# Second layer's feed-forward: seventeen weight panels as seven half-size products instead of eight, sums on GpSimd

## The reference

```python
D_FF_2 = 2816            # 22 panels of 128 gate and 128 value columns

def swiglu(t, w_in, w_out):
    a, b = jnp.split(t @ w_in, 2, axis=-1)
    return (jax.nn.silu(a) * b) @ w_out

x = x + g2 * swiglu(modulate(rmsnorm_2(x, norm2_g[i]), sh2, sc2), ffn_w_in[i], ffn_w_out[i])
```

## Time and profile before

| | |
|---|---|
| median of three runs | 2506.89 us (2505.44 to 2507.58) |
| the profiled execution | 2507.14 us, span 2505.8 us |
| TensorE busy | 2472.0 us, 99% of the span |
| VectorE, ScalarE busy | 1508.1 us (60%), 988.9 us (39%) |
| GpSimd busy | 136.7 us (5%) |
| mean granted clock of TensorE | 0.996 |

### The profile page before, as it was taken

How to read it: one execution, slowest core, us unless ns; L and a number is a source line. 1 busy time by engine, 2 the same in 40 slices (tenths; PEclk the granted TensorE clock), 3 DMA queues, 4 the chain that set the end, 5 groups by cost and what they waited for, 6 DMA issues and landing times.

```text
span 2505.8 us, 32300 instructions
## 1 busy us (share of the span) xinstructions
PE 2472.0 (99%) x13178; PEld 2052.0 (82%) x13178; DVE 1508.1 (60%) x2618; ACT 988.9 (39%) x1985; POOL 136.7 (5%) x148
## 2 busy tenths in 40 slices
PE   8999999999999999999999999999999999999998
PEld 6888888778888788888888788888888888888887
DVE  8787753555666557766665288676644644633434
ACT  6543242453354442333522377432223423422222
POOL 1000000000010010000122000100000001000001
PEclk9999999999999999999999999999999999999999
DMA  4221012212333144654212100366632222222222
GB/s 148 85 84 35 18 52 93 93 68 76 126 135 124 62 185 169 235 202 151 93 67 85 51 1 18 141 226 230 221 113 87 102 101 94 92 101 101 97 84 72
DMA packets 39941, 270.33 MB, mean 108 GB/s; under 512 B 4336, under 2 KB 4592, under 8 KB 9072
## 3 DMA queue, kind: packets, MB, share of 16 engines
q1 hardware_dynamic: 30064, 206.71, 23.0%
q0 software_dynamic: 9040, 60.33, 6.6%
q10 hardware_dynamic: 688, 1.22, 0.1%
HBM read 266.14 MB, written 2.10 MB: 107 GB/s over the span
## 4 chain that ended last, share of the span: by engine, by line
PE 94%; DVE 4%; ACT 2%; issue 0%; DMA 0%; DVEq 0%; ACTq 0%; POOLq 0%
PE bank L142 91%; PE bank L145 2%; DVE w_lo L151 1%; ACT tmp L148 0%; DVE dd L151 0%; DVE x_t L159 0%; DMA kept_consts<-in_consts 0%; DVE tmp L151 0%; DVE change L159 0%; ACT w_hi L148 0%; ACT da_p L148 0%; ACT L148 0%; DVE dd L145 0%; DVE da_stat L168 0%; DVE low L151 0%
## 5 line engine op out<-in xcount | busy, mean ns | idle before, releaser
L142 PE MATMUL bank<-h_hi,w_hi 128*128 128x512 f32 x1824 | 694.5, 395 | 0.1
L142 PE MATMUL bank<-h_lo,w_hi 128*128 128x512 f32 x1824 | 677.1, 390 | 0.0
L151 DVE TENSOR_TENSOR w_lo<-w_raw,w_hi 128x512 fp32r<-128x512 f32 (+3 forms) x746 | 490.8, 713 | 140.0 <-ACT w_hi L148 139.5
L142 PE MATMUL bank<-h_hi,w_lo 128*128 128x512 f32 x1824 | 570.7, 390 | 0.0
L148 ACT ACTIVATE w_hi<-w_raw 128x512 fp32r<-128x512 f32 (+3 forms) x746 | 426.6, 637 | 334.9 <-PE bank L142 321.3
L142 PEld LDWEIGHTS bank<-h_lo,w_hi 128*128 128x128 f32 x1824 | 342.2, 188 | 72.4 <-DVE h_lo L159 0.8
L142 PEld LDWEIGHTS bank<-h_hi,w_hi 128*128 128x128 f32 x1824 | 342.4, 188 | 70.2 <-issue 0.8
L142 PEld LDWEIGHTS bank<-h_hi,w_lo 128*128 128x128 f32 x1824 | 341.4, 188 | 68.2
L142 PE MATMUL bank<-f_hi,w_hi 128*128 128x512 f32 x816 | 315.6, 390 | 0.2 <-DVE w_lo L151 0.2
L142 PE MATMUL bank<-f_lo,w_hi 128*128 128x512 f32 x816 | 300.1, 389 | 0.0
L142 PE MATMUL bank<-f_hi,w_lo 128*128 128x512 f32 x816 | 270.3, 389 | 0.0
(11 more groups left out here) (383 smaller groups left out, 3004.4 us busy)
## 6 DMA issues: line engine op xcount, KB each, us to landing
w_raw<-in_pack_ffn SPq DMA_DIRECT2D x60, 1024.0 KB, 4.8
ada_w<-in_ada_w POOLq DMA_DIRECT2D x48, 1024.0 KB, 5.1
w_raw<-in_pack_mlp SPq DMA_DIRECT2D x32, 1024.0 KB, 4.9
w_raw<-in_pack_gdn_qkv SPq DMA_DIRECT2D x12, 1024.0 KB, 4.7
w_raw<-in_pack_sc_cu SPq DMA_DIRECT2D x8, 1024.0 KB, 4.7
w_raw<-in_pack_ffn SPq DMA_DIRECT2D x8, 768.0 KB, 4.2
w_raw<-in_pack_gdn_z SPq DMA_DIRECT2D x4, 1024.0 KB, 4.7
w_raw<-in_pack_gate_a SPq DMA_DIRECT2D x4, 1024.0 KB, 4.8
```

Source lines behind the costliest of these rows:

```text
L142: return self.engine.matmul(*a, **k) if self.engine is not None else self
L151: return self.engine.tensor_tensor(*a) if self.engine is not None else self
```

## The change

In panels 5 to 21 of the second layer's first product, the block product of a 2 x 2 arrangement (row blocks 0 to 3 and 4 to 7, gate and value columns, first and second 256 tokens) is formed from seven products of half size (`m1` to `m7`), in the manner of Strassen and Winograd, where the plain form has eight. Each is four row blocks by three matmuls of 256 columns, into one half of a PSUM bank; four banks serve a panel. The weights' seven forms are the four quarters that occur as they are (the first piece of 1024 columns holds two, the second of 512 one) and four sums, made by GpSimd in `w_sums` (`seven_sums_pool`) and split like the others: six pieces in place of four. The input's sums `t_sums` are made once, by GpSimd (`seven_forms_pool`), and split into `t_hi` and `t_lo` by ScalarE and VectorE during panels 1 to 3. The four quarters of the result are put together by adds: five on VectorE from PSUM, two on GpSimd, two copies on ScalarE. The hidden tile of a panel is finished during the next one. The plain panels 0 to 4 and the whole first layer stay as they were.

```diff
+    PIECES, SEVEN_PIECES, SEVEN_FROM = 4, 6, 5
...
+        if j == 0:
+            parts = [w[n % 2][:, 0:2 * T].rearrange("p (k m) -> p k m", k=DT) for w in (w_hi, w_lo)]
+            return raw[:, :, 0:P], parts
...
+    def seven_lo_piece(V, n, j):
+        src, (hi, lo) = seven_piece(n, j)
+        V.wait_ge(*at("act_hi", (n, j)))
+        V.tensor_tensor(lo, src, hi.bitcast(F32), ALU.subtract).then_inc(
...
+    def seven_sums_pool(G, n, before):
...
+        for j, (out, a, b, op) in enumerate(((s1, a21, a22, ALU.add), (s2, s1, a11, ALU.subtract),
+                                             (s3, a11, a21, ALU.subtract), (s4, a12, s2, ALU.subtract))):
+            if before is not None:
+                G.wait_ge(*at("dve_lo", (before, j + 2)))
...
+        if i == SEVEN_FROM:
+            T_.wait_ge(*at("dve_seven", ("t", 3)))
+        T_.wait_ge(*at("dve_lo", n))
...
+            for k in range(4):
+                T_.matmul(out, hi[:, k, :], b_hi(k), start=(k == 0), stop=False)
+                T_.matmul(out, lo[:, k, :], b_hi(k), start=False, stop=False)
+                done = T_.matmul(out, hi[:, k, :], b_lo(k), start=False, stop=(k == 3))
...
+    def seven_forms_pool(G):
+        a, b = sq[0], sq[1]
+        for k in range(4):
+            for t, tile in ((a, k), (b, 4 + k)):
+                G.wait_ge(*at("act_h_hi", ("ffn1", tile)))
+                G.wait_ge(*at("dve_h_lo", ("ffn1", tile)))
...
+                G.tensor_tensor(t[:, :], h_hi[:, tile, :].bitcast(F32), h_lo[:, tile, :].bitcast(F32), ALU.add).then_inc(
...
+            if k:
+                G.wait_ge(*at("dve_seven", ("t", k - 1)))
+            G.tensor_tensor(t_sums[:, 0, :], a[:, second_half], a[:, first_half], ALU.subtract).then_inc(
...
+            if behind is not None:
+                corner(behind)
+            piece()
+            if behind is not None:
+                product(behind)
+            add(i, "u2", s1, "m6", "b", 0, u2, at("act_seven", ("s1", i)), *made)
+            piece()
+            if behind is not None:
+                rest(behind)
+            piece()
+            add(i, "c11", s1, "m2", "c", 0, seven_a[:, first_half])
+            piece()
+            add(i, "u3", u2, "m7", "d", 0, u3, at("dve_seven", ("u2", i)), *made, frees=True)
+            piece()
+            piece()
+            add(i, "c21", u3, "m4", "b", 1, seven_b[:, first_half], at("dve_seven", ("u3", i)), frees=True)
...
+        for i, following in zip(SEVEN, SEVEN[1:] + [None]):
+            beside_it = following is not None and block_of(following) == block_of(i)
+            if beside_it:
+                seven_sums_pool(G, seven_n(following), seven_n(i))
+            corners(i)
```

More of the change, by code:

```diff
@@ L468, in panel_size, with in_seven, pieces_of, form_of @@
         return nk * width
-    PIECES = 4
+    PIECES, SEVEN_PIECES, SEVEN_FROM = 4, 6, 5
+    def in_seven(n):
+        return n < len(order) and order[n][0] == "ffn1_1" and order[n][2] >= SEVEN_FROM
+    def pieces_of(n):
+        return SEVEN_PIECES if in_seven(n) else PIECES
+    def form_of(parts, n, j):
+        whole, more = parts
+        if j < 4:
+            return whole[n % 2][:, T * j:T * (j + 1)]
+        return more[n % 2][:, j - 4, :]
+    def seven_piece(n, j):
+        raw = w_raw[n % 2][:, :].rearrange("p (k m) -> p k m", k=DT)
+        if j == 0:
+            parts = [w[n % 2][:, 0:2 * T].rearrange("p (k m) -> p k m", k=DT) for w in (w_hi, w_lo)]
+            return raw[:, :, 0:P], parts
+        parts = [form_of(w, n, j + 1) for w in ((w_hi, more_hi), (w_lo, more_lo))]
+        if j == 1:
+            return raw[:, 4:8, P:2 * P], [part.rearrange("p (k m) -> p k m", k=4) for part in parts]
+        return w_sums[j - 2][:, :], parts
@@ L591, in gemm_beside @@
                 for k in range(nk):
-                    if piece is not None and steps < PIECES:
+                    if piece is not None and steps < pieces_of(ahead):
                         piece(lane, ahead, steps)
@@ L3362, in hidden_before, with seven_place @@
         return ("pe_tile", (f"ffn1_{layer}", 0, 0, 1))
+    SEVEN_BLOCKS = [[i for i in range(max(k0, SEVEN_FROM), k0 + nk)] for k0, nk in FFN_BLOCKS]
+    SEVEN = [i for panels in SEVEN_BLOCKS for i in panels]
+    seven_n = lambda i: number["ffn1_1", 0, i]
+    block_of = lambda i: i // 8
+    hidden_of = lambda i: (1, i // 8, i % 8)
+    first_half, second_half = slice(0, HT), slice(HT, T)
+    def seven_place(place, i, half):
+        return bank_of((place, i))[:, HT * half:HT * (half + 1)]
@@ new lines, in seven_scalar, with tanh, hidden, piece @@
+    def seven_scalar(S, panels):
+        def tanh(i):
+            S.wait_ge(*at("dve_seven", ("c12", i)))
+            S.wait_ge(*at("dve_ffn", ("lo", *hidden_of(i - 1))))
+            S.activation(seven_y[:, :], seven_a[:, :], ACT.Tanh, scale=0.5).then_inc(*up("act_seven", ("tanh", i)))
+        def hidden(i):
+            layer, blk, f = hidden_of(i)
+            S.wait_ge(*at("dve_ffn", ("product", layer, blk, f)))
+            S.wait_ge(*at(*hidden_before(layer, blk)))
+            S.activation(f_hi[:, f, :], seven_y[:, :], ACT.Copy).then_inc(*up("act_ffn", ("hi", layer, blk, f)))
+        for i in panels:
+            ahead, before = seven_n(i) + 1, seven_before(i)
+            pieces = iter(range(pieces_of(ahead)))
+            def piece():
+                j = next(pieces, None)
+                if j is not None:
+                    split_hi_piece(S, ahead, j)
+            behind = None if i == panels[0] else i - 1
+            piece()
+            if behind is not None:
+                tanh(behind)
+            S.wait_ge(*(at("dve_seven", ("c12", before)) if before else at("dve_ffn", ("lo", 1, 0, i - 2))))
+            S.wait_ge(*at("pe_tile", ("m1", i)))
+            S.activation(s1, seven_place("a", i, 0), ACT.Copy).then_inc(*up("act_seven", ("s1", i)))
+            piece()
+            if behind is not None:
+                hidden(behind)
+            piece()
+            piece()
+            if before is not None:
+                S.wait_ge(*at("pool_seven", ("c22", before)))
+            S.wait_ge(*at("pe_tile", ("m5", i)))
+            S.activation(s5, seven_place("a", i, 1), ACT.Copy).then_inc(*up("act_seven", ("s5", i), frees=("a", i)))
+            piece()
+            piece()
+        tanh(panels[-1])
+        hidden(panels[-1])
@@ new lines, in seven_vector, with add, corner, product @@
+    def seven_vector(V, panels):
+        def add(i, name, left, product, place, half, out, *waits, frees=False):
+            V.wait_ge(*at("pe_tile", (product, i)))
+            for wait in waits:
+                V.wait_ge(*wait)
+            V.tensor_tensor(out, left, seven_place(place, i, half), ALU.add).then_inc(
+                *up("dve_seven", (name, i), frees=(place, i) if frees else None))
+        def corner(i):
+            add(i, "c12", v_part, "m3", "c", 1, seven_a[:, second_half], at("pool_seven", ("v", i)), frees=True)
+        def product(i):
+            layer, blk, f = hidden_of(i)
+            V.wait_ge(*at("act_seven", ("tanh", i)))
+            V.scalar_tensor_tensor(seven_y[:, :], seven_y[:, :], 1.0, seven_a[:, :], ALU.add, ALU.mult).then_inc(
+                *up("dve_seven", ("silu", i)))
+            V.wait_ge(*at("dve_seven", ("silu", i)))
+            V.wait_ge(*at("pool_seven", ("c22", i)))
+            V.scalar_tensor_tensor(seven_y[:, :], seven_y[:, :], 0.5, seven_b[:, :], ALU.mult, ALU.mult).then_inc(
+                *up("dve_ffn", ("product", layer, blk, f)))
+        def rest(i):
+            layer, blk, f = hidden_of(i)
+            V.wait_ge(*at("act_ffn", ("hi", layer, blk, f)))
+            V.tensor_tensor(f_lo[:, f, :], seven_y[:, :], f_hi[:, f, :].bitcast(F32), ALU.subtract).then_inc(
+                *up("dve_ffn", ("lo", layer, blk, f)))
+        for i in panels:
+            ahead, before = seven_n(i) + 1, seven_before(i)
+            pieces = iter(range(pieces_of(ahead)))
+            def piece():
+                j = next(pieces, None)
+                if j is not None:
+                    split_lo_piece(V, ahead, j)
+            behind = None if i == panels[0] else i - 1
+            made = [at("pool_seven", ("c22", before))] if before is not None else []
+            if behind is not None:
+                corner(behind)
+            piece()
+            if behind is not None:
+                product(behind)
+            add(i, "u2", s1, "m6", "b", 0, u2, at("act_seven", ("s1", i)), *made)
+            piece()
+            if behind is not None:
+                rest(behind)
+            piece()
+            add(i, "c11", s1, "m2", "c", 0, seven_a[:, first_half])
+            piece()
+            add(i, "u3", u2, "m7", "d", 0, u3, at("dve_seven", ("u2", i)), *made, frees=True)
+            piece()
+            piece()
+            add(i, "c21", u3, "m4", "b", 1, seven_b[:, first_half], at("dve_seven", ("u3", i)), frees=True)
+        corner(panels[-1])
```

(2 more changed lines are left out.)

123 lines of the change are left out of this document (116 added, 7 removed).

## The result

The kernel after takes 2525.24 us (median of 4 runs, 2524.35 to 2528.97), the kernel before 2506.16 beside it (2504.43 to 2507.58): a ratio of 1.0079, 95% interval 1.0062 to 1.0097. It is 0.8% slower, where 2527 was forecast. The profiled execution spans 2524.8 us, 19.0 more than that of before.

A forecast was written before the change was run, and what follows sets the result against it. The prediction took TensorE to bound the kernel before, and VectorE with GpSimd's holds the changed panels. 2507.14 + 8.1 (panels) + 11.9 (start) = 2527 us, 0.8% slower; range 2496 to 2548.

The forecast's parts named there:

- The heart: VectorE instructions with two SBUF inputs and GpSimd ones exclude each other; a 512-column GpSimd instruction holds VectorE 1.15 us.
- contended panel: One of eleven seven-product panels, neither first nor last of its block, with weight sums made beside it: 12.0 us, formerly 10.88.
- The panels' sum: Panels 5 to 21: eleven at 12.0, three firsts at 10.3, three lasts at 10.08, 193.1 against 185.0: +8.1 us.
- The start's sum: Start of the second layer: making input forms, then panel 5's weight sums and pieces, delays panel 5 by 11.9 us.
- 3.2 us of late `h_lo`: Panel 1 of the second layer: forms' instructions delay the normalised input's low parts, felt as 3.2 us and passed on.
- The cover by PSUM adds: VectorE's five half-width adds from PSUM, 2.1 us a panel, lie beside GpSimd's holds and hide that much of them.
- my formula: VectorE's time per panel: its queue plus GpSimd's holds less its PSUM adds, 8.3 + (5.8 - 2.1) = 12.0 us.
- the sign: In panels 9 to 14, `w_lo` pieces of 512 columns would take 1.0 to 1.7 us, GpSimd adds 1.6 to 1.8.
- The port doesn't matter: Rival, 18%: GpSimd's sums slip into gaps, all 17 panels take 10.08 us, the start stays hidden: 2493.5 us.
- Half of it: Rival, 12%: the start is mostly hidden, a contended panel takes about 11.2 us: 2507 within 5 us.
- GpSimd is dearer: Rival, 10%: reading weights in runs of 128 makes a hold 1.65 us, a panel 14.5, the start +18: 2561 us.
- Weight loads bind: Rival, 1%: at half width TensorE's weight loads of 0.188 us set the panel at 15.8 us: +84 us.

The follow-up runs named there:

- e1: Kernel after, with GpSimd's weight sums beside another seven-product panel replaced by blanks (zeros written, nothing read, results wrong): 2508.75 us.
- e2: Kernel after, with one more 448-column GpSimd add behind the corner sums wherever another seven-product panel stands beside: 2536.52 us.
- e5: Kernel after, with the 14 sets of weight sums beside other seven-product panels moved from GpSimd to VectorE, behind its first piece: 2516.95 us.
- e6: Kernel after, with GpSimd starting the activations' forms only when VectorE has done with the layer's first panel: 2526.58 us.
- e8: On top of e7, seven products only in panels 8 to 21, forms spread over panels 2 to 5, GpSimd's part after the first panel: 2500.58 us.
- e9: Kernel after, with seven products only from panel 8 on and the activations' forms spread over panels 2 to 5: 2512.94 us.
- e3: Kernel after, with two 448-column GpSimd blanks (no SBUF read) in the place of e2's added add: 2531.16 us.
- e4: Kernel after, with both corner sums moved from GpSimd to VectorE, taking product m5 from PSUM, and ScalarE's copy of m5 dropped: 2516.27 us.
- e10: On top of e8, first and fourth weight sums of the third and later panels of a block moved from GpSimd to VectorE: 2497.73 us.
- e7: On top of e4, ScalarE applies SiLU itself in the seven-product panels, so one VectorE multiplication falls away: 2510.49 us.

## Why the prediction was right, step by step

**The heart held.** VectorE's work with two SBUF inputs and GpSimd's reads of SBUF exclude each other, and that is what a contended panel costs: 11.76 us against 12.0 forecast. Of panel 11's 11.77 us of VectorE, the holds are 3.98 (worked out below), so its own queue is 7.8, not 8.3: after an add out of PSUM the next instruction starts 0.33 us later, not 0.42. The holds net of cover were put at 3.7; these two errors cancel in part. e1 takes away the reads of the sums, and the panel falls to 10.45; e2 adds one read and it grows by 0.97; e5 moves the sums into VectorE's queue, and it falls to 11.02. The rule of the Trainium skill (SBUF — State Buffer, "Who interferes with whom") names as the other party a GpSimd instruction that reads SBUF, not one that only writes it; e1 agrees (0.68 us for the silu step beside a blank, against 1.78 beside a sum in the kernel after).

**The panels' sum** came to 8.8 us against 8.1, with two errors that cancel. Contended panels were a little cheaper: three second ones at 11.88 or 11.89 and eight at 11.76 make 129.7, not 132. The firsts of blocks 2 and 3 took 10.56 (forecast 10.3), the lasts 10.06 (10.08, so the 0.120 a product held). Panel 5, put at 10.3 as the first of its block, took 12.69.

**The step that I left out: the clock.** TensorE stood for 7 us before panel 5, which I had forecast, and I priced only the standing. The granted clock then was 0.50 for the first 5 us of the panel, where 24 weight loads start 0.213 us apart instead of 0.120. This is about 2.1 us on top of the 10.56 of the other two first panels (8 and 16). In the seven experiments that start at panel 5 it was 1.4 to 2.4. The forecast had no term for it, and the panels' sum came near only because the contended ones were cheaper by as much.

**The start's sum** was near, 12.6 against 11.9, and its later steps came out where they were put: counted from panel 1's first weight load, panel 5's weight sums begin at 45.1 us and end at 52.1, against 44.3 and 50.9 forecast. (Two slips of 0.1 us in that sum cancel, 2188.8 and 6.7 for 2188.9 and 6.6, and its 0.53 us for a VectorE piece stands in no row; 0.62 does.) But one of its terms is wrong: that 3.2 us of late `h_lo` "is certain" and "every later one hangs on it". TensorE did wait there, 4.2 us, 0.4 of it as before. e6 takes this wait away and panel 5 is no earlier, since the first quarter of the forms waits anyway for its place in ScalarE's list. So the sum was near by luck: without the 3.2 it gives 8.7, and which later term is too small by the rest isn't shown. The chain can be hidden: with three panels more and one quarter of the forms per panel the cost is 0.5 us (e8, e9); which of the two does it wasn't tried apart.

**The cover by PSUM adds** I counted whole, 2.1 us a panel. e3 and e4 show that it depends on the order: it is worth only what of a GpSimd read lies beside such an add. That the kernel after came near it is luck of its order: in panel 11 the held instructions are 0.42 + 1.09 + 0.97 + 0.77 + 0.73 = 3.98 us longer than alone, against 5.8 - 2.1 = 3.7 in my formula. About half of it fell on the two silu steps, not on the weight pieces that I had named as the sign. In e4 the same formula gave 10.8 and the steady panel took 11.46.

**The rivals.** *The port doesn't matter*: excluded by the rows and e1. *Half of it*: the panel was not at 11.2 and the start not hidden. *GpSimd is dearer*: its sum over runs of 128 takes 1.30 in e4 (at 2325.75), like the 1.29 of the earlier trace rows. *Weight loads bind*: 84 products in 10.1 to 10.2 us exclude it.

**What stays open.** Whether a start at panel 5 could be hidden by another order of the forms wasn't tried. How much of e10's 2.9 us below e8 is the moved sums isn't settled by the times: their intervals overlap. The two profiled executions speak for the sums: from panel 8 to the end e10 takes 233.35 us, e8 236.25, and the waits for `seven_lo` fall from 4.3 to 1.3.

## What to carry to other kernels

When work goes to an idle GpSimd, don't add up the queues one by one: add what VectorE does with two SBUF inputs to what GpSimd reads, and count as free only what stands beside adds from PSUM or blanks. If VectorE has little slack, a sum in its own queue (0.61 us for 512 columns) is cheaper than one beside it (a hold of up to 1.1 us, less only where it meets adds from PSUM). And a change with a set-up should begin where the set-up has room: here the start cost 12.6 us and the panels 8.8, and with the start nearly free and the contention reduced the same seven products beat the eight, by 0.2 to 0.3%.

## What the runs showed that I had not expected

A stall of TensorE can cost more than its length. In the kernel after, 7 us without a product were followed by 5 us at the granted clock of 0.50, the 1.2 GHz level. Much the same came after a shorter stall. In e6 TensorE stood for 2.95 us before panel 4; its windows then (stretch, length, busy, granted clock, DMA):

```profile
2175.50:2178.64 3.14, 0.22 (x1) 1.00 0.00 0
2178.64:2180.60 1.96, 1.93 (x6) 0.61 0.00 0
2180.60:2182.60 2.00, 2.00 (x6) 0.52 0.00 0
2182.60:2185.00 2.40, 2.40 (x12) 1.00 0.35 72
```

The Trainium skill (TensorE: Matmul & The Clock Gate, "Part 1: The HAM clock gate (the "warmup" mystery)") has the rule that the array's clock is halved when it has been idle; these rows agree. But not every stall brings it. After the 1.31 us before panel 4 of the kernel after the clock stayed at 1.00, and so it did in e7 after 2.90 us at the same place, where 2.91 us in e5 brought it to 0.50. The rows of e7:

```profile
2176.00:2179.60 3.60, 0.76 (x4) 1.00 0.00 0
2179.60:2181.60 2.00, 1.94 (x9) 1.00 0.00 0
```

So the length of the stall alone doesn't tell whether the clock falls; what else decides isn't shown.

Moving an instruction that itself holds nobody can cost as much as one that does: the two blanks of e3 displaced a sum from beside PSUM adds, and 0.61 us a panel came of it.
